# The first panel behind two norms as a sum of two panels, joined by the token factor

## What is computed

```python
def rmsnorm(x, g):
    xf = x.astype(jnp.float32)
    y = xf * lax.rsqrt(jnp.mean(xf * xf, axis=-1, keepdims=True) + EPS)
    return (y * g.astype(jnp.float32)).astype(x.dtype)
...
    for l in range(DEPTH):
        n = norm_gains[l]
        h = h + 0.5 * rmsnorm(swiglu(rmsnorm(h, n[0]), ffn1_wi[l], ffn1_wo[l]), n[1])
        h = h + rmsnorm(hybrid_mixer(rmsnorm(h, n[2]), w_in[l], sconv_w[l], dn_conv_w[l],
                                     dn_A_log[l], dn_dt_bias[l], dn_norm[l], w_fourier[l],
                                     w_sconv_out[l], w_dn_out[l], w_out[l]), n[3])
        h = h + 0.5 * rmsnorm(swiglu(rmsnorm(h, n[4]), ffn2_wi[l], ffn2_wo[l]), n[5])
    return h[:, N_META:]
```

## Time and profile before

| | |
|---|---|
| median of 3 runs | 1046.09 us (1043.07 to 1047.61) |
| the profiled execution | 1048.54 us, span 1046.8 us |
| TensorE busy | 1011.4 us, 97% of the span |
| VectorE, ScalarE, GpSimd busy | 555.5, 479.1, 767.1 us |
| mean granted clock of TensorE | 0.984 of full |

### The profile page before, as it was taken

The page is one execution under the profiler, slowest core; times in us unless marked ns, Lnnn a source line. Parts: engine busy times, 40 slices in busy tenths (PEclk is TensorE's granted clock), DMA queues, the critical chain, the costliest instruction groups (busy, mean ns, idle before and its releaser), DMA issues.

```text
span 1046.8 us, 21649 instructions
## 1 busy us (share of the span) xinstructions
PE 1011.4 (97%) x8190; PEld 988.8 (94%) x8190; DVE 555.5 (53%) x1017; ACT 479.1 (46%) x720; POOL 767.1 (73%) x599
## 2 busy tenths in 40 slices
PE   6999999999999999999999999999999999999995
PEld 5899999999999999999899889999999989999995
DVE  4324995547544444734554663466656954444234
ACT  6244223446654444444556633433245465545441
POOL 3396656565989889997486834666539959999993
PEclk9999999999999999999999988999999999999998
DMA  9363434443556555565363123444315636665661
GB/s 341 114 196 115 131 103 124 137 124 101 180 174 198 163 179 174 166 183 160 102 193 109 52 70 101 122 137 126 102 61 175 218 102 194 197 183 180 182 183 55
DMA packets 48298, 154.62 MB, mean 148 GB/s; under 512 B 6028, under 2 KB 11156, under 8 KB 48232
## 3 DMA queue, kind: packets, MB, share of 16 engines
q1 hardware_dynamic: 46080, 151.31, 45.9%
q10 hardware_dynamic: 2152, 2.38, 0.7%
HBM read 151.57 MB, written 2.10 MB: 147 GB/s over the span
## 4 chain that ended last, share of the span: by engine, by line
PE 80%; POOL 6%; DVE 6%; ACT 3%; issue 3%; DMA 1%; SPq 0%; DVEq 0%; ACTq 0%; POOLq 0%
PE panel L1612 62%; POOL wlo L609 6%; PE panel L1659 3%; PE aux L1756 2%; PE panel L1707 1%; PE panel L1695 1%; PE aux L1951 1%; PE aux L1999 1%; PE aux L1988 1%; PE aux L1940 1%; PE aux L2028 1%; PE aux L2037 1%; PE aux L1667 1%; DMA memx<-in_mem 1%; PE aux L2039 1%
## 5 line engine op out<-in xcount | busy, mean ns | idle before, releaser
L609 POOL TENSOR_TENSOR wlo<-raw,whi 128x512 fp32r<-128x512 f32 x552 | 738.1, 1368 | 256.5 <-ACT whi L700 234.2
L1612 PE MATMUL panel<-xh,whi 128*128 128x256 f32 (+1 forms) x1440 | 418.7, 291 | 3.9 <-POOL wlo L609 2.0
L1612 PE MATMUL panel<-xh,wlo 128*128 128x256 f32 (+1 forms) x1440 | 410.3, 285 | 0.0
L1612 PE MATMUL panel<-xl,whi 128*128 128x256 f32 (+1 forms) x1440 | 409.7, 285 | 0.0
L700 ACT ACTIVATE whi<-raw 128x1024 fp32r<-128x1024 f32 x276 | 289.9, 1053 | 198.9 <-PE panel L1612 165.2
L1612 PEld LDWEIGHTS panel<-xh,whi 128*128 128x128 f32 x1440 | 272.9, 190 | 6.2 <-issue 5.2
L1612 PEld LDWEIGHTS panel<-xh,wlo 128*128 128x128 f32 x1440 | 272.8, 189 | 0.0
L1612 PEld LDWEIGHTS panel<-xl,whi 128*128 128x128 f32 x1440 | 272.2, 189 | 0.6
L1612 PE MATMUL panel<-hh,wlo 128*128 128x272 f32 (+1 forms) x352 | 100.4, 285 | 0.0
L1612 PE MATMUL panel<-hh,whi 128*128 128x272 f32 (+1 forms) x352 | 100.1, 284 | 0.0
L1612 PE MATMUL panel<-hl,whi 128*128 128x272 f32 (+1 forms) x352 | 99.9, 284 | 0.0
(11 more groups left out here) (312 smaller groups left out, 1594.4 us busy)
## 6 DMA issues: line engine op xcount, KB each, us to landing
raw<-in_panels SPq DMA_DIRECT2D x228, 512.0 KB, 3.5
raw<-in_down SPq DMA_DIRECT2D x32, 448.0 KB, 3.2
raw<-in_down SPq DMA_DIRECT2D x16, 512.0 KB, 3.5
memk<-in_mem_panels SPq DMA_DIRECT2D x4, 512.0 KB, 7.8
memv<-in_mem_panels SPq DMA_DIRECT2D x4, 512.0 KB, 13.4
memx<-in_mem SPq DMA_DIRECT2D x4, 256.0 KB, 5.6
h<-in_x SPq DMA_DIRECT2D x1, 1024.0 KB, 8.3
spill<-h ACTq DMA_DIRECT2D x1, 1024.0 KB, 6.3
```

What stands on the lines that cost most here:

```text
L609: ins = nc.gpsimd.tensor_tensor(wlo[:, slot, half], raw[:, slot, half], whi[:, slot, half].bitcast(f32), ALU.subtract)
L1612: ins = M(bank[:, 0:w], wt[:, slot, P * t:P * t + P], x[:, kk, c0:c0 + w], start=first and m == 0 and n == 0, stop=last and m == len(pairs ...
```

## The change

For norms 4 and 6 the first panel behind the pre-norm no longer waits for the new h. With the gain of the post-norm g, its token factor r, the unnormed output y and the gain of the pre-norm g', the new h is h + r (c g y), and the panel W on g' h is W (g' h) + r W (g' c g y). So:

- ScalarE and VectorE split g' h into ah and al, `EARLY` says beside which output: for norm 4 two tiles each beside the first four, for norm 6 one each beside outputs 1 to 5, two beside the sixth, one beside the seventh (the numbers count from 0). They split b = g' c g y into bh and bl, output by output.
- ScalarE now squares each output straight from its bank and VectorE takes it out with g and c on it (`take_out`), which also carries ScalarE's whi; ScalarE waits for VectorE's tmp before bh.
- TensorE makes the first panel with `output_apart`: the sum over partitions of the first seven squares, three blocks on ah and al, the sum with the last square, four blocks more, 24 matmuls on bh and bl into a bank of its own, the last block on ah and al. No fillers are left at norms 4 and 6. `first_outputs` then takes panels 1 and 2 (ABREAST = 3).
- VectorE's `join` multiplies the second bank by rstd and adds it to the first.
- The combine has one product and one sum, on tiles singly or in pairs (PAIRS, QUARTERS), since g and c are in tmp already.
- GpSimd splits panel 3 behind the norm without waiting for xl, and VectorE splits panel 4 (`low_panel`), whose whi ScalarE makes inside the pre-norm.
- The spill's reload is issued behind the delta norm, and the tables for logarithm and exponential are loaded ahead of DOWN1's outputs, and ahead of OUT2's first whi.
- At norm 8 the same `take_out` without b; the combine in pairs, and four stores of 256 KB.

```diff
-ABREAST = 2
+ABREAST = 3
+PAIRS = [(0,), (1,), (2, 3), (4, 5), (6, 7)]
+QUARTERS = [(0, 1), (2, 3), (4, 5), (6, 7)]
...
+        ah = at("ah", ar + 13056, [P, KT, LEN], f32r)
+        al = at("al", ar + 13056 + KT * LEN, [P, KT, LEN], f32r)
+        bh = at("bh", ar + 13056 + 2 * KT * LEN, [P, KT, LEN], f32r)
+        bl = at("bl", ar + 13056 + 3 * KT * LEN, [P, KT, LEN], f32r)
...
+        APART = {4: 0, 6: 1, 8: 2}
+        TILES = {4: PAIRS, 6: PAIRS, 8: QUARTERS}
+        WEIGHED = {4: 0, 6: len(PAIRS), 8: 2 * len(PAIRS)}
+        EARLY = {4: [(0, 1), (2, 3), (4, 5), (6, 7), (), (), (), ()],
+                 6: [(), (0,), (1,), (2,), (3,), (4,), (5, 6), (7,)], 8: [()] * 8}
...
-            for half in range(2):
-                sp.wait_ge(h_ready, 8 * 3 + 4 * half + 4)
-                sp.dma_start(a["out"][:, 4 * half:4 * half + 4, :], h[:, 4 * half:4 * half + 4, META:LEN]).then_inc(stored, 16)
-            sp.wait_ge(stored, 32)
+            for t, u in QUARTERS:
+                sp.wait_ge(h_ready, tile_done(8, u))
+                sp.dma_start(a["out"][:, t:u + 1, :], h[:, t:u + 1, META:LEN]).then_inc(stored, 16)
+            sp.wait_ge(stored, 16 * len(QUARTERS))
...
-            pool.wait_ge(split_low, 8 * SPLIT[5] + 8)
+            ahead(MIX_P)
+            skip(MIX_P + 4)
...
+                    if kk == 5:
+                        ahead(nxt[0] - LEAD)
...
+            def take_out(first_o, first_p, each, n, at0, following=None):
+                w = W[n]
+                for i in range(KT):
+                    ahead(first_p + each * i + each - 1)
+                    for t in EARLY[n][i]:
+                        A(ah[:, t, 0:w], h[:, t, hcol(w)], ACT.Identity, scale=vcol("gains", at0 + 8 + t)).then_inc(a_high, 1)
+                    o = first_o + i
+                    out_wait(o)
+                    if i == KT - 1 and following is not None:
+                        ahead(following)
+                    A(sq[:, i, 0:w], pb[o % 4][:, 0:w], ACT.Square).then_inc(down_squared, 1)
+                    if following is not None:
+                        bank_freed(act, o)
+                        A(bh[:, i, 0:w], tmp[:, i, 0:w], ACT.Identity, scale=vcol("gains", at0 + 8 + i)).then_inc(b_high, 1)
...
-            with act.Fori(0, 2) as g:
-                for n in range(12):
-                    high_in_loop(g, 12, n)
-            nxt[0] += 24
             nc.scalar.preload_act_table_set(LN_EXP)
+            act.wait_ge(h_ready, 8)
+            take_out(DOWN1_O, DOWN1_P, 3, 4, 8, MIX_P)
             post_root(4)
-            pre_norm(5, combined(1), "gains", 16, DOWN1_O + 7)
+            pre_norm(5, combined(4), "gains", 16)
...
-            act.wait_ge(yc_ready, 4)
-            act.dma_start(h[:, :, META:LEN], a["spill"]).then_inc(h_back, 16)
-            for o in range(8):
-                ahead(OUT2_P + o)
-            ahead(UP2_P)
+                    act.wait_ge(yc_ready, 4)
+                    act.dma_start(h[:, :, META:LEN], a["spill"]).then_inc(h_back, 16)
             nc.scalar.preload_act_table_set(LN_EXP)
+            act.wait_ge(h_back, 16)
+            take_out(OUT2_O, OUT2_P, 1, 6, 24, UP2_P)
             post_root(6)
-            pre_norm(7, combined(2), "gains", 32, OUT2_O + 7)
+            pre_norm(7, combined(6), "gains", 32)
             pre_root(7)
             up_loop(1, UP2_O, ROWS)
-            ahead(PANELS - 1)
             nc.scalar.preload_act_table_set(LN_EXP)
+            take_out(DOWN2_O, DOWN2_P, 3, 8, 40)
...
-            def combine(n, at0, factor, following=None):
-                w = W[n]
+            def combine(n, at0=0, following=None):
+                w, tiles = W[n], TILES[n]
                 dve.wait_ge(rstd_ready, n + 1)
-                for t in range(KT + 2):
-                    if t < KT:
-                        STT(tmp[:, t, 0:w], tmp[:, t, 0:w], vcol("gains", at0 + t), rstd[:, 0:w], ALU.mult, ALU.mult)\
-                            .then_inc(weighed, 1)
-                    kk = t - 1
-                    if 0 <= kk < KT:
-                        dve.wait_ge(weighed, 8 * (n // 2 - 2) + kk + 1)
-                        STT(h[:, kk, hcol(w)], tmp[:, kk, 0:w], factor, h[:, kk, hcol(w)], ALU.mult, ALU.add).then_inc(h_ready, 1)
-                    kk = t - 2
-                    if following is not None and kk >= 0:
-                        low_part(following, kk, "gains", at0 + 8)
+                for m in range(len(tiles) + 2):
+                    if m < len(tiles):
+                        t = slice(tiles[m][0], tiles[m][-1] + 1)
+                        TT(tmp[:, t, 0:w], tmp[:, t, 0:w], bc(rstd[:, 0:w], 1, len(tiles[m])), ALU.mult).then_inc(weighed, 1)
+                    if 0 < m <= len(tiles):
+                        t = slice(tiles[m - 1][0], tiles[m - 1][-1] + 1)
+                        dve.wait_ge(weighed, WEIGHED[n] + m)
+                        TT(h[:, t, hcol(w)], tmp[:, t, 0:w], h[:, t, hcol(w)], ALU.add).then_inc(h_ready, 1)
+                    if following is not None and m > 1:
+                        for kk in tiles[m - 2]:
+                            low_part(following, kk, "gains", at0 + 8)
...
-            def take_in(first_o, n):
+            def take_out(first_o, n, at0, factor):
+                w = W[n]
                 for i in range(KT):
+                    for t in EARLY[n][i]:
+                        dve.wait_ge(a_high, 8 * APART[n] + t + 1)
+                        STT(al[:, t, 0:w], h[:, t, hcol(w)], vcol("gains", at0 + 8 + t), ah[:, t, 0:w].bitcast(f32),
+                            ALU.mult, ALU.subtract).then_inc(a_low, 1)
                     o = first_o + i
-                    out_wait(o)
-                    y = norm_source(n)[:, i, :]
-                    if n == 2:
-                        TT(y, y, pb[o % 4][:, 0:W[n]], ALU.add).then_inc(bank_free[o % 4], 1)
-                    else:
-                        CP(y, pb[o % 4][:, 0:W[n]]).then_inc(bank_free[o % 4], 1)
-                    bank_freed(dve, o)
-                    ins = TT(sq[:, i, 0:W[n]], y, y, ALU.mult)
-                    if i == KT - 1:
-                        ins.then_inc(last_squared, 1)
-                    elif i:
-                        order(ins)
-                        ins = TT(sq[:, 0, 0:W[n]], sq[:, 0, 0:W[n]], sq[:, i, 0:W[n]], ALU.add)
+                    dve.wait_ge(down_squared, 8 * APART[n] + i + 1)
+                    TS(tmp[:, i, 0:w], pb[o % 4][:, 0:w], vcol("gains", at0 + i), factor, ALU.mult, ALU.mult)\
+                        .then_inc(bank_free[o % 4], 1)
+                    if n < 8:
+                        dve.wait_ge(b_high, 8 * APART[n] + i + 1)
+                        STT(bl[:, i, 0:w], tmp[:, i, 0:w], vcol("gains", at0 + 8 + i), bh[:, i, 0:w].bitcast(f32),
+                            ALU.mult, ALU.subtract).then_inc(b_low, 1)
+                    if 0 < i < KT - 1:
+                        ins = TT(sq[:, 0, 0:w], sq[:, 0, 0:w], sq[:, i, 0:w], ALU.add)
                         if i == KT - 2:
                             ins.then_inc(summed, 1)
                         else:
                             order(ins)
+            def low_panel(p):
+                dve.wait_ge(hi_ready, p + 1)
+                dve.wait_ge(lo_ready, p)
+                TT(wlo[:, p % RING, :], raw[:, p % RING, :], whi[:, p % RING, :].bitcast(f32), ALU.subtract).then_inc(lo_ready, 1)
+            def join(o, n):
+                bank, use = aux("apart", n)
+                w = W[n]
+                aux_wait(dve, use)
+                TT(tmp[:, 0, 0:w], bank[:, 0:w], rstd[:, 0:w], ALU.mult).then_inc(aux_free[use % 4], 1)
+                aux_freed(dve, use)
+                out_wait(o)
+                order(TT(pb[o % 4][:, 0:w], pb[o % 4][:, 0:w], tmp[:, 0, 0:w], ALU.add))
...
-            take_in(OUT2_O, 6)
             dve.wait_ge(h_back, 16)
-            combine(6, 24, 1.0, 7)
+            take_out(OUT2_O, 6, 24, 1.0)
+            combine(6, 24, 7)
+            low_panel(UP2_P + 4)
+            join(UP2_O, 7)
...
-                late = n in (2, 4, 6, 8)
                 aux_open(use)
                 pe.wait_ge(summed, n + 1 if n < 2 else n // 2 + 2)
-                ins = M(bank[:, 0:W[n]], ones[:], y[:, 0, 0:W[n]], start=True, stop=not late)
-                if late:
-                    spare = aux("stat", n + 1) if n < 8 else None
-                    if spare:
-                        aux_open(spare[1])
-                        keep_clock(spare[0], 3)
-                    pe.wait_ge(last_squared, n // 2 - 1)
+                ins = M(bank[:, 0:W[n]], ones[:], y[:, 0, 0:W[n]], start=True, stop=n != 8)
+                if n == 8:
+                    pe.wait_ge(down_squared, 8 * APART[n] + KT)
                     ins = M(bank[:, 0:W[n]], ones[:], y[:, KT - 1, 0:W[n]], start=False, stop=True)
-                    if spare:
-                        ins.then_inc(aux_full, 1)
```

(22 more changed lines are left out.)

36 lines of the change are left out of this document (22 added, 14 removed).

## The result

| | before | after |
|---|---|---|
| median | 1046.08 us (1043.07 to 1047.61) | 1057.58 us (1056.95 to 1061.93) |
| profiled execution | 1048.54 us, span 1046.8 | 1056.95 us, span 1055.0 |

The ratio is 1.0131, 95% interval 1.0106 to 1.0156: slower by 11 to 16 us. The forecast was 1055.5 us, with a range from 1041.5 to 1059.

The account below looks back on a forecast made before the run. The prediction took TensorE, busy 97% of the span, to bound the kernel. Its terms, +9.1 + 2.05 + 0.2 − 1.9 = +9.45 us, gave 1055.5 us from the median of 1046.09, range 1041.5 to 1059.

Parts of the forecast that it names:

- the early al are hidden: DOWN1: outputs lie 8.3 us apart, so making al early there costs nothing; no term.
- OUT2 and the second join: Term from OUT2 through the second join: late al delays the apart panel, +9.1 us (−2.5 to +10.8).
- The ring: OUT2: each turn runs whi, hand-over, one half, al, tmp, bh in a row, 3.75 us against 2.87 for the panel.
- The clock's term: Second join: TensorE stands 8 us or more without fillers, then 3.3 us at half speed lose 1.65 us.
- The first join: Term for the join behind DOWN1: +2.05 us (−0.8 without lock waits and low clock, +4 with longer low stretch).
- The combine starts in effect 1.4 us later: First join: bl(7) and the combine's first operation wait for GpSimd's halves while it splits panel 3; 1.4 us later.
- the panel that was won is panel 2, the cover of the rates' chain: First join: panel 2 no longer covers the rates' chain, so panel 3 starts at 516.2 instead of 515.8.
- The entry into DOWN2: End of UP2: ScalarE waits for DOWN2's first panel before copying the last tile's hh, +0.2 us (0 to 0.5).
- The end: Behind DOWN2: square beside gain, combine on pairs and a smaller last store, −1.9 us (−1.4 to −2.4).
- the clock decides: Rival: al(7) at 846.9 and low stretches twice as long at both joins, +3.3, 1058.8 us; chance 0.10.
- It pays as meant: Rival: OUT2's turn at most a panel long, al(7) by 838, both gaps filled, −5.2 or 1040.9 us; chance 0.20.

Follow-up runs that it names:

- e4: The changed kernel with OUT2's running sum of squares moved from VectorE to TensorE: turn still 3.54 us, ratio 1.0130.
- e6: The changed kernel with bh and bl made from PSUM, scaled by the product of the two gains, at both joins: 1050.84 us, ratio 1.0056.
- e9: The changed kernel with 24 filler products behind OUT2 and 4 more behind the sum at the second join: ratio 1.0105.
- e5: The changed kernel with bh and bl of each output of OUT2 moved one turn later: turn 4.31 us, ratio 1.0107.
- e10: The changed kernel with GpSimd waiting at the first join until VectorE's eight low parts of h are done: ratio 1.0107.
- e1: The kernel before with only the end of the change (square on ScalarE, combine on pairs, four stores): ratio 0.9997.
- e7: The changed kernel with panel 3 ahead of the cumulate products and logits ahead of panel 1's way out of PSUM: 1052.94 us, ratio 1.0069.
- e8: The changed kernel with DOWN1's early ah and al one output later and ScalarE's gains wait behind its second output's splits: 1057.37 us, ratio 1.0119.
- e11: The changed kernel with the edits of e6, e7 and e8 together: 1043.58 us, ratio 0.9983.
- e3: The changed kernel with ScalarE's wait for the eight gains on h moved behind one split more: 1057.52 us, ratio 1.0134.
- e12: e11 with GpSimd pausing at both joins for VectorE's low parts and OUT2's al one per output: 1041.67 us, ratio 0.9958.
- e14: e12 with seven fillers behind OUT2's last product and three behind the sum at the second join: ratio 0.9967.

## Why the prediction was right or wrong

The direction, the place and the mechanism of the largest term held. Two steps failed in size, and both are around DOWN1 and the first join. The forecast had no term for DOWN1, on the ground that "the early al are hidden"; it measured +2.06 us. And it had +2.05 for the first join, which measured +3.95. Together they are 4.0 us short. The second join came out 1.1 us below its term, so the sum is too low by less, 9.45 against 12.1 us by the stretches: part of its closeness is luck.

**OUT2 and the second join, forecast +9.1, measured +8.0.** The ring was named right, and e4 to e6 show it: turn 3.54 us for a forecast 3.75 (the parts overlap by some tenths, since the next instruction starts 0.40 us behind one listed with 0.47), al 1.15 us. That al(7) was done at 847.8 for a forecast 846.9 is two differences that nearly cancel: the changed kernel enters OUT2 2.1 us later than the one before, and from OUT2's first product to al(7) it takes 33.1 us, where the forecast amounts to 34.3. Without the clock the join cost 7.3 us (e9) for a forecast 7.5. The clock's term was mis-sized: I took 1.65, and 1.6 us of slow products were there, but half of it was hidden behind the wait for xl, so it cost 0.75. What I had not seen is e5: the ring hides a second bound of 4.3 us.

**The first join, forecast +2.05, measured +3.95.** Three sub-steps came out larger. "The combine starts in effect 1.4 us later": its first two operations each waited for a half, 2.9 us instead of 0.8, and the abreast panels ended 3.0 us later in the join, not 1.9 (e10 gives 1.8 back). From their end to panel 3 it took 9.5 us for a forecast 9.2, so panel 3 starts 1.86 us later in the join instead of 0.4. And from panel 3 on 2.1 us were lost at the low clock instead of 1.65. The forecast took the slow stretch of the kernel before to follow from the wait of 1.72 us in front of it; e1 has the same wait and a clock of 1.00, so this wait does not decide it by itself, and what does stays open. The step "the panel that was won is panel 2, the cover of the rates' chain" was right, and e7 shows it to be the largest lever here.

**DOWN1, no term, measured +2.06.** The sentence that failed is "The outputs here are 66 products or 8.3 us apart, so the early al are hidden". They are not. ScalarE's wait for VectorE's eight gains on h stands in front of the first ones, and ScalarE waits a second time for tmp, which stands behind two al on VectorE; behind both waits is the whi that GpSimd needs. I priced what each engine adds to its work there, and not what is queued behind the added waits. e6 takes away the second wait alone and gives 1.4 us back; e8 moves the gains' wait and the early al and gives 1.5; with both (e11) DOWN1 is 66.17 us, 0.1 above the kernel before. e3 moved the gains' wait by one split only and kept the stall.

**The entry into DOWN2, forecast +0.2**, is two-valued, and what decides between the two values stays open. It is 0 in the changed kernel, e3 and e8 to e10 (62.44 or 62.45), and 0.85 to 1.05 in the seven others that keep the longer lead (63.29 to 63.48); in e4 it is this row of TensorE:

```profile
990.09 0.36 PE L1660 MATMUL panel<-hh,whi 128*128 128x256 f32 x1 [0.80 <-DVE hl L1358]
```

**The end, forecast −1.9, measured −1.9**, and the same in e1.

**The rivals.** The measured time is near "the clock decides" (1058.8), and its condition came true: the slow stretches at both joins were 6.8 us long, twice the 3.4 of the kernel before. Its price did not: it counts 3.3 us for each join, and 2.1 and 0.75 were lost, since TensorE stood in part of the slow stretches. That the total comes near it is luck; what makes up the difference is the unpriced DOWN1 and the combine's waits. "It pays as meant" put its deciding point at al(7) by 838, which is 25.4 us behind OUT2's first product in the kernel before. In e12 and e14 it is 26.5 us, 3.1 behind the start of OUT2's last product, and they lose 1.3 us and nothing at that join. Its price of −2.5 us is reached in no run.

## What to carry to other kernels

Where a change adds a wait to an engine, list what is queued behind it before pricing what it adds, other engines' feeds above all: here two waits on ScalarE emptied GpSimd, and TensorE paid. Before breaking a ring of hand-overs, work out what each engine does per turn once nobody stands; a second bound may lie behind the first, and only an edit that serves both (here reading the operand from PSUM) pays. And work pulled forward into a gap is taken from somewhere: look at what it covered there. And compare the granted clock of the two traces stretch by stretch before reading a difference of a microsecond or two as the edit's.

## What the runs showed of the hardware

- The waits of VectorE and GpSimd for each other are lopsided. An operation of VectorE with two SBUF inputs waits for the half in progress (1.1 to 1.5 us instead of 0.4 to 0.5), the same operation with one input in PSUM does not (0.47 us in e6), and GpSimd loses little: two halves with one al between them take 2.71 us, 0.19 more than 2 x 1.26. This is less than the whole 0.4 us that the exclusive lock of the Trainium skill (SBUF — State Buffer, Who interferes with whom) would take from it.
- The middle, which is alike in all kernels but for the reload's place, varied by 3.6 us between them.
- In e12 TensorE stood 1.6 and 0.7 us, with a sum between them, ahead of the window below, which has 0.78 of the clock; with ten fillers there (e14) it was 1.00 over the same products. But a wait does not settle it: with the same 1.72 us in front of the logits' transposes join 1 had a slow stretch of 3.4 us in the kernel before and none in e1.

```profile
833.80:841.50 7.70, 7.70 (x50) 7.51 (x51) 4.42 (x11) 2.63 (x7) 2.22 (x2) 0.78 0.45 139
```
